# Down projections: both parts of the gated products move against one weight load

## The reference

```python
def _swiglu(h, w_up, w_down):          # w_up 1024 x 5632, w_down 2816 x 1024
    gu = h @ w_up
    g, u = jnp.split(gu, 2, axis=-1)
    return (jax.nn.silu(g) * u) @ w_down

x = x + 0.5 * gate(0) * _swiglu(norm_mod(x, 0), w_ffn_up[l, 0], w_ffn_down[l, 0])
```

## Time and profile before

| | |
|---|---|
| median of three runs | 1593.21 us |
| profiled execution, its own time | 1594.71 us |
| span of its trace | 1592.9 us |
| granted TensorE clock, mean over the span | 0.998 |
| TensorE matmuls, busy | 1558.1 us (98%), 13290 |
| VectorE, busy | 1285.8 us (81%), 1933 |
| ScalarE, busy | 905.1 us (57%) |
| GpSimd, busy | 240.4 us (15%) |
| DMA, share of 16 engines | 70.9% on the weight queue |

### The profile page before, as it was taken

The page is one execution under the profiler, slowest core; times in us unless marked ns, Lnnn a source line. Parts: engine busy times, 40 slices in busy tenths (PEclk is TensorE's granted clock), DMA queues, the critical chain, the costliest instruction groups (busy, mean ns, idle before and its releaser), DMA issues.

```text
span 1592.9 us, 32431 instructions
## 1 busy us (share of the span) xinstructions
PE 1558.1 (98%) x13290; PEld 1533.4 (96%) x13290; DVE 1285.8 (81%) x1933; ACT 905.1 (57%) x1563; POOL 240.4 (15%) x254
## 2 busy tenths in 40 slices
PE   4999999999999999999999999999999999999998
PEld 3999999999999999999999999999999999999998
DVE  6788898888888878888887898788888888786553
ACT  5455457665554655459665445667555466664553
POOL 4122000022210222000112231001221010021100
PEclk9999999999999999999999999999999999999999
DMA  9999974459888889864569998434899873457761
GB/s 342 345 335 336 324 273 156 162 189 347 311 315 283 291 304 326 295 231 153 185 226 332 314 318 270 163 132 147 305 333 335 312 243 130 141 190 238 237 215 41
DMA packets 110996, 403.11 MB, mean 253 GB/s; under 512 B 12562, under 2 KB 12818, under 8 KB 110720
## 3 DMA queue, kind: packets, MB, share of 16 engines
q1 hardware_dynamic: 109280, 395.87, 70.9%
q0 software_dynamic: 1568, 5.17, 1.2%
HBM read 399.94 MB, written 1.05 MB: 252 GB/s over the span
## 4 chain that ended last, share of the span: by engine, by line
PE 87%; DVE 8%; ACT 2%; issue 1%; DMA 1%; SPq 0%; DVEq 0%; ACTq 0%
PE PS L558 86%; DVE SCR L1695 2%; DVE WL L1692 2%; DVE SCR L1692 1%; DMA SCR<-in_x 1%; ACT WH L1216 1%; DVE SCR L2049 1%; DVE ring L1718 1%; DVE SMALL L2048 1%; ACT SCR L1503 0%; PE PS L1159 0%; PE PS L1055 0%; DVE MOD L1689 0%; DVE SCR L1689 0%; DVE SMALL L2088 0%
## 5 line engine op out<-in xcount | busy, mean ns | idle before, releaser
L1692 DVE TENSOR_TENSOR WL<-ring,WH 128x1024 fp32r<-128x1024 f32 (+1 forms) x508 | 604.2, 1223 | 184.7 <-ACT WH L1216 184.4
L558 PE MATMUL PS<-HH,WH 128*128 128x256 f32 (+1 forms) x2640 | 628.7, 280 | 2.2 <-ACT WH L1216 2.2
L558 PE MATMUL PS<-HL,WH 128*128 128x256 f32 (+1 forms) x2640 | 614.8, 277 | 0.0
L1216 ACT ACTIVATE WH<-ring 128x1024 fp32r<-128x1024 f32 (+1 forms) x508 | 511.4, 1049 | 46.8 <-PE PS L558 44.1
L558 PEld LDWEIGHTS PS<-HH,WH 128*128 128x128 f32 x2640 | 496.7, 188 | 3.3 <-ACT WH L1216 2.3
L558 PEld LDWEIGHTS PS<-HL,WH 128*128 128x128 f32 x2640 | 491.7, 188 | 0.6
L558 PE MATMUL PS<-HH,WL 128*128 128x256 f32 (+1 forms) x2640 | 375.8, 278 | 1.0 <-DVE WL L1692 0.7
L1718 DVE CUSTOM_DVE_ANT_0 ring<-ring,CB,VC 128x1024 f32<-128x1024 f32 x238 | 331.1, 1408 | 11.2 <-DMA ring<-in_ada 11.2
L558 PEld LDWEIGHTS PS<-HH,WL 128*128 128x128 f32 x2640 | 337.0, 189 | 1.8 <-DVE WL L1692 1.8
L558 PE MATMUL PS<-AH,WL 128*128 128x256 f32 x1056 | 292.4, 277 | 0.5 <-DVE WL L1692 0.5
L558 PE MATMUL PS<-AH,WH 128*128 128x256 f32 x1056 | 292.6, 277 | 0.0
(11 more groups left out here) (214 smaller groups left out, 1457.4 us busy)
## 6 DMA issues: line engine op xcount, KB each, us to landing
ring<-in_up SPq DMA_DIRECT2D x176, 512.0 KB, 5.7
ring<-in_ada SPq DMA_DIRECT2D x144, 512.0 KB, 6.1
ring<-in_ffn SPq DMA_DIRECT2D x132, 512.0 KB, 4.9
ring<-in_mod SPq DMA_DIRECT2D x96, 512.0 KB, 5.8
ring<-in_down SPq DMA_DIRECT2D x88, 512.0 KB, 5.7
ring<-in_win SPq DMA_DIRECT2D x64, 512.0 KB, 5.7
ring<-in_wout SPq DMA_DIRECT2D x32, 512.0 KB, 4.2
ring<-in_winv SPq DMA_DIRECT2D x8, 512.0 KB, 4.2
```

Of the source, the lines that this page charges most:

```text
L558: return e.matmul(out, lhsT, rhs, start=start, stop=stop, skip_group_check=skip)
L1216: e.activation(half_of(i)[0], slot_of(("half", i, 0))[:, 0:w], ACT.Copy).then_inc(s_hi, 1)
L1692: return e.tensor_tensor(out, a, b, op)
```

## The change

`AH` and `AL` become one tensor `AHL` in which the two parts of a depth k lie side by side, 256 and 256 columns. For chunks 0 to 6 the two matmuls on `WH` become one that moves the 512 columns of `AHL[:, k]` into the whole bank: WH·AH is summed in columns 0 to 255, WH·AL in columns 256 to 511. The matmul on `WL` adds to columns 0 to 255 as before. `residual` then adds the two halves of the bank to X one after the other, the first with `step`, and the second tells of the chunk. Chunk 7 keeps three matmuls of 256 columns and one addition. The up stage, the mixers and all DMAs are as before.

```diff
-        AH = nc.alloc_sbuf_tensor_at("AH", [128, NF, S], F32R, offset=scr_at)
-        AL = nc.alloc_sbuf_tensor_at("AL", [128, NF, S], F32R, offset=scr_at + 4 * NF * S)
+        AHL = nc.alloc_sbuf_tensor_at("AHL", [128, NF, 2, S], F32R, offset=scr_at)
+        AH, AL = AHL[:, :, 0, :], AHL[:, :, 1, :]
@@ out_proj, TensorE
-                    mm(out, wh[:, g, :], xh(k), start=k == 0, stop=False)
-                    mm(out, wh[:, g, :], xl(k), start=False, stop=False)
+                    if c < KD - 1:
+                        mm(PS[:, down_bank(n, c), :], wh[:, g, :], AHL[:, k, :, :].rearrange("p a s -> p (a s)"),
+                           start=k == 0, stop=False, skip=True)
+                    else:
+                        mm(out, wh[:, g, :], xh(k), start=k == 0, stop=False)
+                        mm(out, wh[:, g, :], xl(k), start=False, stop=False)
                     if g == 0:
                         e.wait_ge(s_lo, h + 1)
-                    last = mm(out, wl[:, g, :], xh(k), start=False, stop=k == kt - 1)
+                    last = mm(out, wl[:, g, :], xh(k), start=False, stop=k == kt - 1, skip=c < KD - 1)
@@ residual, VectorE
-                stt(X[:, c, :], PS[:, down_bank(n, c), 0:256], MOD[:, 24 * n + 16 + c:24 * n + 17 + c], X[:, c, :], ALU.mult,
-                    ALU.add).then_inc(s_x, 1)
+                gate = MOD[:, 24 * n + 16 + c:24 * n + 17 + c]
+                if c < KD - 1:
+                    step(stt(X[:, c, :], PS[:, down_bank(n, c), 256:512], gate, X[:, c, :], ALU.mult, ALU.add))
+                stt(X[:, c, :], PS[:, down_bank(n, c), 0:256], gate, X[:, c, :], ALU.mult, ALU.add).then_inc(s_x, 1)
```

## The result

The changed kernel takes 1607.27 us (median of five runs, 1606.59 to 1607.55) against 1593.21 for the kernel before (five runs, 1592.84 to 1599.55). The ratio is 1.0074, with a 95% interval from 1.0055 to 1.0092. I had forecast 1595.2 us in a range of 1588.0 to 1602.0, so the time lies above the range. The profiled execution took 1607.5 us, with a span of 1605.7 us: 12.8 more than the span before. (The medians differ by 14.1 us; the profiled execution of the kernel before is 1.5 above its median.)

What follows compares the result with a forecast made beforehand. TensorE was taken as the bound, by the number of matmuls times what 256 moved columns cost, with VectorE second. TensorE 0 plus VectorE 2.0 us on 1593.2 us made 1595.2 us, range 1588.0 to 1602.0.

Steps and rivals of the forecast that it cites:

- the pitch of 512 columns: TensorE in the down stages: 924 wide matmuls at 226.7 ns each, twice 113.3, so no change in time.
- The bound of 235 from the earlier trace: Upper bound in ns for a 512-column matmul, from matmuls in pairs; it would make TensorE's part 7.7 us more.
- Long matmuls run at the slower pitch: Rival, chance 0.19: 512-column matmuls in down stages keep the slower pace, 7.7 us on top, 1602.4 us.
- The test that I had set: Down stages: a depth should take 340 ns; the forecast is wrong under 337 or over 343 ns.
- If they are paid once per instruction: Rival, chance 0.33: 6.6 ns fixed per matmul, 512 columns at 219.9 ns; TensorE saves 6.2 us, giving 1591.5 us.
- VectorE's part: Down stages: 42 more additions, each with a wait for its own end, cost 2.0 us, between 0 and 4.3.
- a wait for WL near 200 us: First down stage: VectorE writes the weights' rests late, so TensorE waits 1.46 us.
- my 1.92: First down stage: the additions of chunks 1 to 4 make VectorE late by 1.92 us.
- The stages at 446 and 627: Down stages where a wait of TensorE for WL was forecast at under 0.3 us.
- Layout and banks: Down stages: writing AHL at another distance and using banks whole cost nothing.

Runs made afterwards that it cites:

- e3: The changed kernel with the wide matmuls but without the second addition (WH x AL missing from the output for chunks 0 to 6): 1606.7 us, ratio 1.008.
- the grouped kernel: The whole change, but the 512-column matmuls of a half of weights run first, up to eight, their remainders behind: 1599.66 us, ratio 1.0031 to the kernel before.
- e2: Kernel before with the new layout, three 256-column matmuls per depth, WH x AL going to columns 256 to 511, and two additions: 1598.04 us, ratio 1.0017.
- e1: Kernel before with the new layout alone, three 256-column matmuls per depth and one addition: 1594.12 us, ratio 1.000.

## Why the prediction was wrong

**The step that failed is the pitch of 512 columns.** "I take 226.7, no change: it is twice the pitch of the same operands in the same stream." It measured 235. The bound of 235 from the earlier trace rows came out, and the reason for which I set it aside ("they ran outside a dense stream") does not hold: the dense stream has it too. That it came out to the nanosecond is partly luck: it doubles the price of 256 more columns in a pair, while the pairs' own starts are 316 and 321 ns apart. By the term's own formula 924 x 8.3 = 7.7 us, not 0.

**The rival that had it was too cheap.** *Long matmuls run at the slower pitch* named the mechanism, with the right 7.7 us, and got a chance of 0.19 and 1602.4 us. It priced the wide matmuls alone. Left out was what their pace does to the 256-column ones: (924 + about 300 of the last chunks) x 4.4 to 4.7 ns, some 5.5 us, which one wide chunk at the front showed by itself. With the 0.6 us of the additions, 7.7 + 5.5 + 0.6 = 13.8 us; the fourth stage had already lost 2.0 of that in the profiled execution before (62.36 - 59.73 - 0.62), and 11.8 remain, as in the table. The earlier trace rows held the other half too: its matmuls stand 11 us behind the stall that slowed them, so a pace stays. I asked which pace a wide matmul takes, and not which pace it leaves. The test that I had set, a depth over 343 ns, came out at 353.

**"If they are paid once per instruction" fell as well.** This rival got 0.33. The excess does not grow in step with the columns, as the widths show, but 256 columns in the quick pace don't have it. So widening a matmul buys an excess instead of saving one.

The Trainium skill gives in TensorE: Matmul & The Clock Gate, section Back-to-back issue gap, the columns at 2.4 GHz and a fixed 2.5 ns for a warm matmul; for 512 columns that is an estimated 216 ns. The prediction left out that the section calls this the gap of an isolated matmul and gives some 131 ns at 512 columns for a stream of weight loads and matmuls. This kernel's stream shows 235, or 232.5 in a row, and agrees with neither; the measurement decides.

**VectorE's part was the smaller error.** I had 2.0 us, of which 1.46 in a wait for WL near 200 us. The wait came where I had put it and for the reason given, but as 0.18 us, or 0.27 with the slower start behind it (62.33 - 62.06). Timelines of the kernel after, VectorE's write and TensorE's weight load, in brackets its idle time and releaser:

```profile
200.87 2.35 DVE L1696 TENSOR_TENSOR WL<-ring,WH 128x1024 fp32r<-128x1024 f32 x2
...
202.14 0.19 PEld L558 LDWEIGHTS PS<-AHL,WL 128*128 128x128 f32 x1 [0.34 <-DVE WL L1696]
```

The rests are written 2.75 us later than at 198.12, but TensorE comes 2.24 us later than at 199.90 too, since its own matmuls are slower. Counted from the start of the stage the rests are 2.40 us later than before, and in e3, which has the wide matmuls without the additions, 1.47 later. So the additions made 0.93 us of lateness and not my 1.92: chunk 0's fell into idle time as I had said (1.21 us are left of it ahead of chunk 1's pair at 172.24, which is 1.00 us long), and ahead of chunk 4 the slower matmuls give VectorE 1.06 us of idle time (e3, at 194.83) where I had counted 0.18. In the grouped kernel, where a stage is 1.3 us shorter, the first stage loses 61.21 - 60.75 = 0.46 us. Within the stages the additions cost 0.57 us in all (376.23 less 375.66): 0.27 in the first, 0.29 in the fourth, none in the fifth, where I had 1.46, 0.25 and 0.25. With the old matmuls their price stays open between nothing and 4.8 us (e2). The stages at 446 and 627 have no wait, as forecast. Layout and banks cost nothing that the stages show, as forecast.

**What stays open.** Why 256 columns have a quick pace and none of the seven other widths has; what makes a stream settle in one pace or the other behind a stall or a rise of the clock; why 384 columns leave the quick pace and two end it at 41 us, while two led to the quick one in a down stage; and the 0.35 us ahead of the first stage.

## What to carry to other kernels

Before fewer and longer instructions are priced, read the pitch of the short ones at both of its values, and ask whether the short form has a pace of its own that the long one will break, and for how long behind it. One foreign instruction near the head of a dense stream cost 7 us here, half of what the change of the whole stream did, so the place of an edit can matter more than its count. Where a kernel's times fall into two groups, compare the pitch of the dense stretches in a run of each before anything else; here one matmul of 0.2 us took the upper group away, and another of two columns took the lower one.

## What the runs showed that I had not expected

- Streams of fp32r matmuls of 256 columns have two paces at the same granted clock of 1.00, 113.3 and 117.7 ns; a pace lasted for over 1500 matmuls (e1, 39 to 222 us).
- Every other width tried, moved alone, takes 3 to 9 ns over the 0.4427 ns per column of the quick 256; 512 columns take 226 once and then 230 to 236; behind a lone 512 the 256s stay slow, behind eight of them they recover in one or two.
- The pace of the first block was settled within six matmuls of the step from 213 ns (clock 0.50) to the 2.4 GHz level, and a slow one cost some 7 us.
- Eight clearings on GpSimd from 920.44 on held a VectorE operation on 8 elements per partition for 4.29 us (0.16 with the clearings spread), and the matmuls behind the stall that followed stayed slow for 50 us in this execution and quick in three others.
